# The input projection of a hybrid decoder trunk: one fp32 product becomes three float32r products, and the first tile follows the weights' pieces

## The chip, the cores and the metric

The kernel runs on one core of a Trainium2 chip. A core has five engines that run their own queues and meet at semaphores: TensorE (PE; its weight loads are shown apart as PEld), VectorE (DVE), ScalarE (ACT), GpSimd (POOL) and SyncE (SP, which here only issues transfers). The metric is the device time of one execution in microseconds. It is 4939.12 us before (median of three, 4939.12 to 4946.64).

## The reference, cut to what matters

One decoder layer runs over 2072 rows (16 meta tokens, 2048 prompt tokens, 8 sample rows). All rows first pass a layer norm and one projection:

```python
h = layer_norm(x, ln_emb_g, ln_emb_b)          # rows x 1024
qa, ka, va, qi, ki, wi, qb, kb, vb, fl = split(h @ w_in)   # 1024 x 2000
# then: rotary on qa, ka, qi, ki; log_sigmoid(fl + b_forget); cumulative sums of it
# sparse attention (indexer, top 256), forgetting attention, output product, gated feed-forward
```

The change is in `h @ w_in` alone. All arithmetic is float32 in the reference.

## The kernel before, in words

The program has five stages, each a block of its own with all engines meeting at its end: `project`, `attend`, `decode`, `mix_out`, `feed_forward`. The feed-forward stage already forms its products from operands split in two float32r parts (`three`, lines 1437 to 1442), as the changed projection does; the projection before uses plain fp32.

`project` walks over 17 tiles of 128 rows (`tiles`: tiles 0 and 1 written out, a hardware loop over pairs, and the last one). For a tile t:

- SP loads its rows to `x_in` once tile t-2 has left DVE (`x_free`) and its rows are stored (`h_stored`). At the start SP also loads `w_in` in eight pieces of 128 x 2000 (1 MB each), straight to their place, all issued in one go (line 203).
- DVE makes the layer norm (`norm`, lines 376 to 391), one tile ahead of the products.
- PE turns the normed rows (`turn_h`, eight transposes to `pT`), ACT copies them out (`copy_h`, line 354, to `hT`), and PE forms four chunks of 500 columns (`pP`), each the sum of eight products over the contraction (line 306). Behind chunk 1 stands `forget_sum` and behind chunk 2 `turn_q`, both for the tile before; behind chunk 3 stands `turn_h` for the next tile.
- ACT copies each chunk to `pn` (line 335), then `copy_h` of the next tile, then an Exp and a Ln (lines 342 and 344), with table loads.
- DVE adds the forget bias (`z`, `az`), applies the rotary steps (lines 427 to 432), and ends with line 434, which waits for ACT's Ln; that end is `lf_done` and `x_free`. `augment` (lines 393 to 404) comes behind the next norm; `turn_q` waits for it and for POOL's copies.
- POOL stores the normed rows, `pn` and the turned queries and keys.

So at a tile's boundary PE waits for ACT's `copy_h` of the next tile, and for nothing else; in tile 0 it waits for all eight pieces of the weights (`w_here`). Order within each engine is the order of the code.

Of the kernel before, what the change touches and what calls it, by code (L numbers as in the profile page):

```python
# [15 lines left out]
P = 128  # L16
D = 1024
KD = D // P
# [3 lines left out]
TILES = -(-ALL // P)  # L22
# [12 lines left out]
N_IN = 2000  # L35
PROJ_CHUNKS = 4
PROJ_W = N_IN // PROJ_CHUNKS
# [52 lines left out]
def project(nc, X, RT, W_IN, LN_G, LN_B, BF, CONST, PN, QTA, QTB, KTD, HN, keep):  # L90

    ident, ones = keep["ident"], keep["ones"]
    with ExitStack() as ctx:
        def sb(name, shape, dt=F32):
            return ctx.enter_context(nc.sbuf_tensor(name, shape, dt))

        def sem(name):
            return ctx.enter_context(nc.semaphore(name))  # L100

        w_in = sb("w_in", [P, KD, N_IN])
        tri = sb("tri", [P, P])
        kT = sb("kT_out", [P, 4, P])
        g_emb = sb("g_emb", [P, D])
# [1 line left out]
        bf = sb("bf", [P, HEADS])  # L107
        x_in = [sb(f"x_in{p}", [P, D]) for p in range(2)]
        rt = [sb(f"rt{p}", [P, 2 * ROPE]) for p in range(2)]
        hT = [sb(f"hT{p}", [P, KD, P]) for p in range(2)]  # L110
        pn = [sb(f"pn{p}", [P, N_IN]) for p in range(2)]
        rope_a = sb("rope_a", [P, 2, 9, ROPE])
        rope_b = sb("rope_b", [P, 2, 9, ROPE])
# [15 lines left out]
        pT = ctx.enter_context(nc.psum_tensor("pT", [P, 2, 512], F32))  # L129
        pP = ctx.enter_context(nc.psum_tensor("pP", [P, 4, 512], F32))  # L130
        pQ = ctx.enter_context(nc.psum_tensor("pQ", [P, 2, 512], F32))
        c_ps = pT[:, 0, 0:HEADS]

        w_here = sem("w_here")
        consts_here = sem("consts_here")
        x_here = [sem(f"x_here{p}") for p in range(2)]
        x_free = sem("x_free")
# [1 line left out]
        sd_done = sem("sd_done")  # L139
        h_done = sem("h_done")  # L140
        hT_ps = sem("hT_ps")
        hT_done = sem("hT_done")
        proj_ps = sem("proj_ps")
        pn_done = sem("pn_done")
        az_done = sem("az_done")
# [39 lines left out]
        @block.sync  # L185
        def _(sp):
            sp.dma_start(g_emb[:], LN_G.unsqueeze(0).to_broadcast([P, D])).then_inc(consts_here, 16)
            sp.dma_start(b_emb[:], LN_B.unsqueeze(0).to_broadcast([P, D])).then_inc(consts_here, 16)
            sp.dma_start(bf[:], BF.to_broadcast([P, HEADS])).then_inc(consts_here, 16)
            sp.dma_start(ident[:], CONST[0]).then_inc(consts_here, 16)  # L190
            sp.dma_start(tri[:], CONST[1]).then_inc(consts_here, 16)
            sp.dma_start(ones[:], CONST[2]).then_inc(consts_here, 16)

            def load(t, p, i):

                if not (isinstance(t, int) and t < 2):
                    wait_alone(sp, x_free, t - 1)
                    wait_alone(sp, h_stored[p], 16 * i)
                sp.dma_start(x_in[p][:], X[ds(t * P, P), :]).then_inc(x_here[p], 16)
                sp.dma_start(rt[p][:], RT[ds(t * P, P), :]).then_inc(x_here[p], 16)  # L200
                if is_first(t):
                    for k in range(KD):
                        sp.dma_start(w_in[:, k, :], W_IN[k * P:(k + 1) * P, :]).then_inc(w_here, 16)

            tiles(sp, load)

# [47 lines left out]
        @block.tensor  # L254
        def _(pe):
            def turn_h(t, p):

                pe.wait_ge(h_done, t + 1)
                if not is_first(t):
                    pe.wait_ge(hT_done, t)  # L260
                if not (isinstance(t, int) and t < 2):
                    pe.wait_ge(aug_done, t - 1)
                for k in range(KD):
                    ins = pe.transpose(pT[:, k // 4, (k % 4) * P:(k % 4 + 1) * P], x_in[p][:, k * P:(k + 1) * P], ident[:])
                ins.then_inc(hT_ps, 1)

            def turn_q(t, p):

                pe.wait_ge(kdup_done, t + 1)
                pe.wait_ge(aug_done, t + 1)  # L270
                for b in range(5):
                    if is_first(t) and b < 2:
                        pass
                    else:
                        pe.wait_ge(q_evac, t * 5 + max(b - 1, 0))
                    out = pQ[:, b % 2, :].rearrange("p (c n) -> p c n", c=4)
                    for c in range(4):
                        if b == 0:
                            ins = pe.transpose(out[:, c, :], pn[p][:, QA + c * P:QA + (c + 1) * P], ident[:])
                        elif b == 1:  # L280
                            ins = pe.transpose(out[:, c, :], pn[p][:, QI + c * P:QI + (c + 1) * P], ident[:])
                        elif b == 2 and c < 2:
                            ins = pe.transpose(out[:, c, :], kdup[:, c, :, :].rearrange("p a b -> p (a b)"), ident[:])
                        elif b == 2:
                            ins = pe.transpose(out[0:AUG, c, :], k_aug[:, c - 2, :], ident[:])
                        else:
                            ins = pe.transpose(out[0:AUG, c, :], q_aug[:, (b - 3) * 4 + c, :], ident[:])
                    ins.then_inc(q_ps, 1)

            def forget_sum(t, p):  # L290

                pe.wait_ge(lf_done, t + 1)

                pe.wait_ge(hT_done, TILES if is_last(t) else t + 2)
                pe.matmul(c_ps, tri[:], pn[p][:, FL:FL + HEADS], start=True, stop=False)
                pe.matmul(c_ps, ones[:], lf_sum[:], start=False, stop=True).then_inc(c_sum_ps, 1)

            def tile(t, p, i):
                pe.wait_ge(hT_done, t + 1)
                for j in range(PROJ_CHUNKS):  # L300
                    if not is_first(t):
                        pe.wait_ge(pn_done, (t - 1) * PROJ_CHUNKS + j + 1)
                    for k in range(KD):
                        if is_first(t) and j == 0:
                            pe.wait_ge(w_here, 16 * KD)
                        ins = pe.matmul(pP[:, j, 0:PROJ_W], hT[p][:, k, :], w_in[:, k, j * PROJ_W:(j + 1) * PROJ_W],  # L306
                                        start=(k == 0), stop=(k == KD - 1))
                    ins.then_inc(proj_ps, 1)
# [12 lines left out]
            turn_q(LAST, 0)  # L321

        @block.scalar
        def _(act):
# [25 lines left out]
            def copy_h(t, p):  # L350
                act.wait_ge(hT_ps, t + 1)
                if not (isinstance(t, int) and t < 2):
                    act.wait_ge(proj_ps, (t - 1) * PROJ_CHUNKS)
                act.activation(hT[p][:].rearrange("p a b -> p (a b)"), pT[:].rearrange("p a b -> p (a b)"),  # L354
                               ACT.Copy).then_inc(hT_done, 1)

            def copy_q(t):
                if not is_first(t):
# [9 lines left out]
            act.wait_ge(pool_init, 1 + HEADS)  # L368
            root(0)
            copy_h(0, 0)  # L370
            tiles(act, tile)
            copy_q(LAST)

        @block.vector
        def _(v):
            ch = Chain(v, dve)

            def norm(t, p, turn):
                v.wait_ge(x_here[p], 32 * (turn + 1))
                layer_norm_stats(ch, x_in[p], stats[:], mv[:])  # L380
                v.sem_inc(var_done, 1)
                v.wait_ge(sd_done, t + 1)
                ch.step(v.reciprocal(rs[:], sd[:]))
                ch.wait()
                ch.step(v.tensor_scalar(x_in[p][:], x_in[p][:], mv[:, 0:1], rs[:], ALU.subtract, ALU.mult))
                ch.wait()
                ch.step(v.tensor_tensor(x_in[p][:], x_in[p][:], g_emb[:], ALU.mult))
                ch.wait()
                ch.step(v.tensor_tensor(x_in[p][:], x_in[p][:], b_emb[:], ALU.add))
                ch.wait()  # L390
                v.sem_inc(h_done, 1)

            def augment(t):

# [14 lines left out]
            def tile(t, p, i):  # L409
# [9 lines left out]
                ch.step(v.scalar_tensor_tensor(out=az[:], in0=z[:], scalar=-1.0, in1=z[:], op0=ALU.mult, op1=ALU.max))  # L419
                ch.wait()  # L420
                v.sem_inc(az_done, 1)

                x4 = [pn[p][:, s:s + 9 * HD].rearrange("p (h d) -> p h d", d=HD) for s in (QA, QI)]
                cos = rt[p][:, 0:ROPE].unsqueeze(1).to_broadcast([P, 9, ROPE])
# [26 lines left out]
            v.wait_ge(consts_here, 96)  # L451
            v.wait_ge(pool_init, 1 + HEADS)
            norm(0, 0, 0)
            per = 2 * (2 + 1 + 4 + 4 + 1 + 1 + 6 + 2 + 1 + 2)
            tiles(v, tile, ch, per)
            augment_last = LAST
# [1918 lines left out]
```

## Time and profile before

| what | value |
| --- | --- |
| time, median of three runs | 4939.12 us (4939.12 to 4946.64) |
| the profiled execution's own time | 4938.44 us |
| its span, first to last instruction | 4936.8 us |
| PE busy | 4234.8 us (86%) |
| DVE / ACT / POOL busy | 2652.9 / 1742.7 / 604.8 us |
| mean granted TensorE clock | 0.917 of full |
| fp32 products of the projection (line 306), PE busy | 469.5 us |

The profile cuts the span in 40 slices of some 123 us. The projection fills nearly the first five: PE is busy 7, 9, 9, 9 and 7 tenths there, and its clock row reads 9 until the projection's end. A row of the trace's timeline reads: start in us, duration in us, engine, line, operation, output <- inputs, shape, count; in brackets how long the engine had been idle, and what ended that. A matmul's duration is a modelled one and overlaps its neighbour's; the distance from one start to the next is the pace. An fp32 product of line 306 leaves two matmul records, a float32r product one.

### The profile page before, as it was taken

To read this page: it belongs to the slowest core of one execution; us is meant where nothing else is said; L and a number is where in the kernel's file an instruction comes from. 1 tells how busy PE (TensorE), PEld (TensorE's weight loads), DVE (VectorE), ACT (ScalarE), POOL (GpSimd) and SP (SyncE) were. 2 spreads that over 40 slices of the span, in tenths; PEclk is the share of its full clock that TensorE was granted. 3 is DMA by queue.
4 is the path that set the end of the run, shared out by engine and by line. 5 is a ranking of instruction groups with operands and counts; after the bars stand their busy time and mean duration, and the time that the engine had idled before them with its cause. 6 is when DMAs were issued, how large, how long until landed. Compare 5 with 4: busy or idle time off the path is not lost. (4 is left out here: it accounts for less than half of the span.)

```text
span 4936.8 us, 61684 instructions
## 1 busy us (share of the span) xinstructions
PE 4234.8 (86%) x23278; PEld 3118.9 (63%) x23278; DVE 2652.9 (54%) x4961; ACT 1742.7 (35%) x2684; POOL 604.8 (12%) x695
## 2 busy tenths in 40 slices
PE   7999748777777888778787798797999999999997
PEld 3444324445555555455546544345999999999997
DVE  2222158989999999998423311343335344353533
ACT  2332223444444445444453344002323233232331
POOL 0221221100000000000167730000000000000000
PEclk9999956888889899999898888898999999999998
DMA  3322220000000000000277751334444534445442
GB/s 131 102 93 84 97 82 31 25 23 16 16 16 16 16 16 9 12 12 5 75 233 216 239 194 35 123 112 119 116 133 125 145 111 125 120 133 141 113 125 71
DMA packets 460722, 444.86 MB, mean 90 GB/s; under 512 B 26728, under 2 KB 405299, under 8 KB 460484
## 3 DMA queue, kind: packets, MB, share of 16 engines
q1 hardware_dynamic: 403396, 256.46, 18.3%
q0 software_dynamic: 57104, 185.42, 11.2%
q8 instruction: 142, 2.33, 0.2%
q14 instruction: 80, 0.66, 0.0%
HBM read 371.71 MB, written 69.95 MB: 89 GB/s over the span
## 5 line engine op out<-in xcount | busy, mean ns | idle before, releaser
L467 DVE TENSOR_SCALAR_CACHE_REDUCE at_relu<-at_scores,at_cand 128x272 f32<-128x272 f32 (+14 forms) x480 | 685.1, 1427 | 9.4
L1440 PE MATMUL ff_ps<-ff_h_high,ff_w_high 128*128 128x412 f32 x1760 | 619.3, 352 | 25.5 <-DVE ff_w_low L1534 25.5
L1441 PE MATMUL ff_ps<-ff_h_low,ff_w_high 128*128 128x412 f32 x1760 | 615.5, 350 | 0.0
L1442 PE MATMUL ff_ps<-ff_h_high,ff_w_low 128*128 128x412 f32 x1760 | 613.2, 348 | 0.0
L306 PE MATMUL pP<-w_in,hT 128*128 128x500 f32 x1088 | 469.5, 587 | 31.0 <-ACT hT L354 19.0
L1534 DVE TENSOR_TENSOR ff_w_low<-ff_w_raw,ff_w_high 128x2048 fp32r<-128x2048 f32 (+1 forms) x150 | 375.6, 2504 | 188.8 <-ACT ff_w_high L1489 188.6
L921 ACT ACTIVATE at_probs<-at_probs,at_nmax 128x144 f32<-128x144 f32 (+15 forms) x256 | 310.9, 1214 | 464.5 <-DVE at_nmax L1003 464.3
L1489 ACT ACTIVATE ff_w_high<-ff_w_raw 128x2048 fp32r<-128x2048 f32 (+1 forms) x150 | 311.5, 2076 | 360.1 <-PE ff_ps L1442 357.9
L934 ACT ACTIVATE at_pT_sb<-tr 128x512 f32<-128x512 f32 x544 | 304.0, 593 | 327.3 <-PE tr L807 326.8
L787 PE MATMUL S<-at_kbT,at_queries_b 73*128 73x512 f32 (+16 forms) x768 | 317.4, 556 | 116.8 <-DVE at_nmax L1003 64.4
L306 PEld LDWEIGHTS pP<-w_in,hT 128*128 128x128 f32 x1088 | 203.8, 191 | 263.4 <-issue 260.7
L807 PE MATMUL tr<-ident,at_probs 128*128 128x128 f32 x2176 | 340.5, 300 | 10.9 <-ACT at_pT_sb L934 5.7
L1440 PEld LDWEIGHTS ff_ps<-ff_h_high,ff_w_high 128*128 128x128 f32 x1760 | 331.1, 188 | 28.3 <-issue 26.2
L1442 PEld LDWEIGHTS ff_ps<-ff_h_high,ff_w_low 128*128 128x128 f32 x1760 | 330.7, 188 | 3.3
L1441 PEld LDWEIGHTS ff_ps<-ff_h_low,ff_w_high 128*128 128x128 f32 x1760 | 330.9, 188 | 0.7
L807 PEld LDWEIGHTS tr<-ident,at_probs 128*128 128x128 f32 x2176 | 278.7, 156 | 82.7 <-ACT at_pT_sb L934 44.8
L787 PEld LDWEIGHTS S<-at_kbT,at_queries_b 73*128 73x128 f32 x768 | 148.5, 215 | 265.8 <-issue 156.4
L1442 PE MATMUL ff_ps<-ff_hid_high,ff_w_low 128*128 128x412 f32 x880 | 308.1, 350 | 0.0
L1441 PE MATMUL ff_ps<-ff_hid_low,ff_w_high 128*128 128x412 f32 x880 | 308.0, 350 | 0.0
L1440 PE MATMUL ff_ps<-ff_hid_high,ff_w_high 128*128 128x412 f32 x880 | 308.0, 350 | 0.0
L2003 ACT ACTIVATE de_kT<-de_tr 128x512 f32<-128x512 f32 (+1 forms) x320 | 177.7, 594 | 330.2 <-PE de_tr L1816 329.4
L787 PE MATMUL S<-at_ka_high,at_q_a 128*128 128x512 f32 (+16 forms) x384 | 159.4, 417 | 132.1 <-DVE at_nmax L1003 128.6
(310 smaller groups left out, 6412.1 us busy)
## 6 DMA issues: line engine op xcount, KB each, us to landing
ff_w_raw<-in_w_gate SPq DMA_DIRECT2D x110, 512.0 KB, 4.0
ff_w_raw<-in_w_up SPq DMA_DIRECT2D x110, 512.0 KB, 5.2
ff_w_raw<-in_w_down SPq DMA_DIRECT2D x80, 704.0 KB, 5.8
out_PN<-pn POOLq DMA_DIRECT2D x17, 1000.0 KB, 6.2
at_q_raw<-dram_QTA SPq DMA_DIRECT2D x124, 128.0 KB, 2.8
x_in<-in_x_rows SPq DMA_DIRECT2D x17, 512.0 KB, 3.8
dram_HN<-x_in POOLq DMA_DIRECT2D x17, 512.0 KB, 8.0
dram_QTA<-qaiT POOLq DMA_DIRECT2D x17, 512.0 KB, 5.3
```

The costliest lines, as they stand in the source:

```text
L306: ins = pe.matmul(pP[:, j, 0:PROJ_W], hT[p][:, k, :], w_in[:, k, j * PROJ_W:(j + 1) * PROJ_W], start=(k == 0), stop=(k == KD - 1))
L467: return v.tensor_scalar(out, x, cand.bitcast(F32), 0.0, ALU.is_ge, ALU.add, accum_out=cnt)
L787: ins = pe.matmul(out[:, lo:lo + w], lhsT, rhs, start=(k == 0), stop=(k == len(passes) - 1))
L807: ins = pe.transpose(tr[state["tb"] % 2][:, h, :], of(h), ident[:])
L921: act.activation(row, row, ACT.Exp, bias=nmax[:, slot:slot + 1], scale=-1.0, accum_out=den[:, slot:slot + 1]).then_inc(exp_done, 1)
L934: act.activation(pT[:, n["pvs"].n % TURNED, :], tr[state["tb"] % 2][:].rearrange("p a b -> p (a b)"), ACT.Copy)\
L1440: pe.matmul(out, w_high[p][:, w], high, start=first, stop=False)
L1441: pe.matmul(out, w_high[p][:, w], low, start=False, stop=False)
L1442: return pe.matmul(out, w_low[p][:, w], high, start=False, stop=last)
L1489: act.activation(w_high[p][:, 0:cols], w_raw[p][:, 0:cols], ACT.Copy).then_inc(w_high_done, 1)
L1534: v.tensor_tensor(w_low[p][:, 0:cols], w_raw[p][:, 0:cols], w_high[p][:, 0:cols].bitcast(F32), ALU.subtract).then_inc(w_low_done, 1)
L2003: act.activation(kT[0:rows, slot, :], tr[0:rows, unit % 2, :], ACT.Copy).then_inc(tr_copied, 1)
```

## The change

- The weights are kept as two float32r parts, `w_high` and `w_low`. A piece is loaded to one of the two `pn` buffers, ACT copies it to `w_high` (a float32r copy), DVE subtracts to make `w_low`; then the buffer takes another piece. So pieces 0 and 1 are loaded at once, and each later piece when DVE has done the one two before it.
- The turned rows are split in the same way: `copy_h` writes `h_high`, and a new DVE step `lower` subtracts `h_high` from `pT` (still in PSUM) into `h_low`. Within a tile `lower(t + 1)` stands behind `az` and ahead of the rotary steps. PE now waits for `h_low_done`.
- Each fp32 product becomes three float32r products (high by high, high by low, low by high).
- In tile 0 the contraction is the outer loop: PE takes a piece for all four chunks as soon as that piece is split. Later tiles keep the chunk as the outer loop.
- In tile 0 the rows of tile 1 are loaded ahead of pieces 2 to 7; DVE and ACT split all the weights before they start tile 1's norm.

```diff
                 if is_first(t):
-                    for k in range(KD):
-                        sp.dma_start(w_in[:, k, :], W_IN[k * P:(k + 1) * P, :]).then_inc(w_here, 16)
+                    for k in range(2):
+                        load_w(k)
+                elif isinstance(t, int) and t == 1:
+                    for k in range(2, KD):
+                        sp.wait_ge(w_low_done, k - 1)
+                        load_w(k)
...
+            def three(p, k, j):
+                out, cols = pP[:, j, 0:PROJ_W], slice(j * PROJ_W, (j + 1) * PROJ_W)
+                pe.matmul(out, h_high[p][:, k, :], w_high[:, k, cols], start=(k == 0), stop=False)
+                pe.matmul(out, h_high[p][:, k, :], w_low[:, k, cols], start=False, stop=False)
+                return pe.matmul(out, h_low[p][:, k, :], w_high[:, k, cols], start=False, stop=(k == KD - 1))
+
             def tile(t, p, i):
-                pe.wait_ge(hT_done, t + 1)
+                pe.wait_ge(h_low_done, t + 1)
+                if is_first(t):
+
+                    for k in range(KD):
+                        pe.wait_ge(w_low_done, k + 1)
+                        for j in range(PROJ_CHUNKS):
+                            ins = three(p, k, j)
+                            if k == KD - 1:
+                                ins.then_inc(proj_ps, 1)
...
+            for k in range(KD):
+                act.wait_ge(w_here[k % 2], 16 * (k // 2 + 1))
+                act.activation(w_high[:, k], pn[k % 2][:], ACT.Copy).then_inc(w_high_done, 1)
+            act.wait_ge(w_low_done, KD)
             tiles(act, tile)
...
+            def lower(t, p):
+                v.wait_ge(h_high_done, t + 1)
+                v.tensor_tensor(h_low[p][:].rearrange("p a b -> p (a b)"), pT[:].rearrange("p a b -> p (a b)"),
+                                h_high[p][:].rearrange("p a b -> p (a b)").bitcast(F32), ALU.subtract).then_inc(h_low_done, 1)
...
                 v.sem_inc(az_done, 1)
+                if not is_last(t):
+                    lower(t + 1, 1 - p)
...
             norm(0, 0, 0)
+            lower(0, 0)
+            for k in range(KD):
+                v.wait_ge(w_high_done, k + 1)
+                v.tensor_tensor(w_low[:, k], pn[k % 2][:], w_high[:, k].bitcast(F32), ALU.subtract).then_inc(w_low_done, 1)
```

On PE, the end of tile 0 and the start of tile 1, before (`pT` takes the turned rows, `pP` the products):

```order
L306 MATMUL pP<-w_in,hT 128x500 x32
L264 MATMUL pT<-ident,x_in 128x128 x8
L306 MATMUL pP<-w_in,hT 128x500 x16
L295 MATMUL pT<-pn,tri 128x8
L296 MATMUL pT<-lf_sum,ones 128x8
L306 MATMUL pP<-w_in,hT 128x500 x8
```

and the same place in the change (each three rows are one product; `hT_high` and `hT_low` are the two parts of the rows):

```order
L314 MATMUL pP<-w_high,hT_high 128x500
L315 MATMUL pP<-w_low,hT_high 128x500
L316 MATMUL pP<-w_high,hT_low 128x500
L278 MATMUL pT<-ident,x_in 128x128 x8
L314 MATMUL pP<-w_high,hT_high 128x500
L315 MATMUL pP<-w_low,hT_high 128x500
L316 MATMUL pP<-w_high,hT_low 128x500
```

The transposes stand where they stood; 32 instructions a tile became 96.

On DVE, the end of tile 0, before:

```order
L417 TENSOR_TENSOR z<-pn,bf 128x8 [waits dve1,pn_done]
L419 SCALAR_TENSOR_TENSOR az<-z 128x8 [waits dve1]
L427 TENSOR_TENSOR rope_a<-pn,rt 128x144 [waits dve1]
L428 TENSOR_TENSOR rope_b<-pn,rt 128x9x8
L429 TENSOR_TENSOR rope_b<-pn,rt 128x9x8
```

and in the change:

```order
L451 TENSOR_TENSOR z<-pn,bf 128x8 [waits dve1,pn_done]
L453 SCALAR_TENSOR_TENSOR az<-z 128x8 [waits dve1]
L424 TENSOR_TENSOR hT_low<-pT,hT_high 128x1024 [waits dve1,h_high_done]
L463 TENSOR_TENSOR rope_a<-pn,rt 128x144
L464 TENSOR_TENSOR rope_b<-pn,rt 128x9x8
L465 TENSOR_TENSOR rope_b<-pn,rt 128x9x8
```

A subtraction of 1024 columns now stands between ACT's copy and PE's products, and ahead of the rotary steps.

On SP, the first loads (`pn` is the buffer that the pieces now pass through), before:

```order
L199 DMA x_in<-in_x_rows 128x1024
L200 DMA rt<-in_rope 128x32
L203 DMA w_in<-in_w_in 128x2000 x8
L199 DMA x_in<-in_x_rows 128x1024
L200 DMA rt<-in_rope 128x32
```

and in the change:

```order
L208 DMA x_in<-in_x_rows 128x1024
L209 DMA rt<-in_rope 128x32
L201 DMA pn<-in_w_in 128x2000 x2
L208 DMA x_in<-in_x_rows 128x1024
L209 DMA rt<-in_rope 128x32
L201 DMA pn<-in_w_in 128x2000 [waits w_low_done] x6
```

Six of the eight pieces now wait for DVE; the rows of tile 1 come ahead of them.

## Rows read from the trace of the kernel before

**Rows 1.** The page's first line: span and instructions.

```profile
span 4936.8 us, 61684 instructions
```

**Rows 2.** Timeline of PE, one tile: start, duration, instruction, [idle before, releaser].

```profile
193.69 13.68 PE L306 MATMUL pP<-w_in,hT 128*128 128x500 f32 x32 [1.20 <-ACT hT L354]
...
224.62 1.04 PE L264 MATMUL pT<-ident,x_in 128*128 128x128 f32 x8
226.86 0.68 PE L306 MATMUL pP<-w_in,hT 128*128 128x500 f32 x1 [1.20 <-ACT hT L354]
```

**Rows 3.** Timeline, ACT and DVE at the end of the same tile.

```profile
225.70 1.02 ACT L354 ACTIVATE hT<-pT 128x1024 f32<-128x1024 f32 x1 [0.28 <-PE pT L264]
...
229.89 0.17 DVE L434 SCALAR_TENSOR_TENSOR pn<-z,sp_l 128x8 f32<-128x8 f32 x1 [2.27 <-ACT sp_l L344]
```

**Rows 4.** Timeline of PEld, fp32 weight loads: first and last of 14.

```profile
208.07 0.19 PEld L306 LDWEIGHTS pP<-w_in,hT 128*128 128x128 f32 x1 [0.23 <-issue]
...
213.52 0.19 PEld L306 LDWEIGHTS pP<-w_in,hT 128*128 128x128 f32 x1 [0.23 <-issue]
```

**Rows 5.** Feed-forward's 412-column products: stretch, length, busy PE PEld DVE ACT, clock, DMA.

```profile
3500.00:3600.00 100.00, 100.00 (x535) 99.45 (x534) 6.41 (x11) 5.67 (x11) 1.00 0.46 123
```

**Rows 6.** Timeline of PE, attention: a 512-column float32r product and the next.

```profile
2407.54 0.39 PE L787 MATMUL S<-at_ka_low,at_q_a 128*128 128x512 f32 x1
2407.77 0.25 PE L787 MATMUL S<-at_ka_high,at_q_a 128*128 128x176 f32 x1
```

**Rows 7.** Instructions of three lines: duration in ns (min/median/max), first and last start, forms.

```profile
L1489 ACT ACTIVATE ff_w_high<-ff_w_raw x150: 1894/1902/2572, 3394.5 to 4878.3; 128x2048 fp32r<-128x2048 f32 x110, 128x2816 fp32r<-128x2816 f32 x40
L1534 DVE TENSOR_TENSOR ff_w_low<-ff_w_raw,ff_w_high x150: 2272/2293/3094, 3397.5 to 4880.9; 128x2048 fp32r<-128x2048 f32 x110, 128x2816 fp32r<-128x2816 f32 x40
L387 DVE TENSOR_TENSOR x_in<-x_in,g_emb x17: 1224/1226/1227, 13.1 to 536.2; 128x1024 f32<-128x1024 f32 x17
```

**Rows 8.** Timeline of the start, to the first product of tile 1.

```profile
15.75 1.94 PE L264 MATMUL pT<-ident,x_in 128*128 128x128 f32 x8 [15.75 <-DVEq L391]
...
17.73 1.02 ACT L354 ACTIVATE hT<-pT 128x1024 f32<-128x1024 f32 x1 [5.74 <-PE pT L264]
29.72 20.66 PE L306 MATMUL pP<-w_in,hT 128*128 128x500 f32 x43 [12.03 <-DMA w_in<-in_w_in]
31.05 1.29 DVE L84 BATCH_NORM_STATS2 stats<-x_in 128x6 f32<-128x512 f32 x2 [15.50 <-DMA rt<-in_rope]
...
35.31 1.23 DVE L389 TENSOR_TENSOR x_in<-x_in,b_emb 128x1024 f32<-128x1024 f32 x1
...
61.17 13.68 PE L306 MATMUL pP<-w_in,hT 128*128 128x500 f32 x32 [1.11 <-ACT hT L354]
```

**Rows 9.** DMA issues: output <- input, queue, count, KB each, us from issue to landing.

```profile
ff_w_raw<-in_w_gate SPq DMA_DIRECT2D x110, 512.0 KB, 4.0
ff_w_raw<-in_w_up SPq DMA_DIRECT2D x110, 512.0 KB, 5.2
...
out_PN<-pn POOLq DMA_DIRECT2D x17, 1000.0 KB, 6.2
...
w_in<-in_w_in SPq DMA_DIRECT2D x8, 1000.0 KB, 13.5
```

**Rows 10.** PE after two idle gaps; stretches: busy PE PEld DVE ACT POOL, clock.

```profile
731.15 0.59 PE L787 MATMUL S<-at_ka_high,at_q_a 128*128 128x272 f32 x1 [2.50 <-DVE at_nmax L1003]
...
2824.97 0.43 PE L1898 MATMUL de_pw<-de_lf_all,de_after 128*128 128x64 f32 x2 [2.38 <-DVE de_lf_all L2151]
...
61.20:594.30 533.10, 497.19 (x1532) 248.47 (x1532) 127.62 (x382) 162.86 (x241) 105.84 (x189) 1.00 0.27 91
...
730.90:737.60 6.70, 4.73 (x28) 3.24 (x28) 6.18 (x29) 2.85 (x9) 0.00 (x0) 0.50 0.00 0
...
2826.70:2830.00 3.30, 3.30 (x18) 3.30 (x17) 1.09 (x5) 0.00 (x0) 2.39 (x4) 0.50 0.91 300
```

**Rows 11.** Timeline of DVE: end of `augment` in the tile of rows 2.

```profile
208.84 0.16 DVE L402 TENSOR_TENSOR lf_sum<-lf_sum,pn 128x8 f32<-128x8 f32 x1
```

More of the change, by code:

```diff
@@ L100, in sem @@
             return ctx.enter_context(nc.semaphore(name))
-        w_in = sb("w_in", [P, KD, N_IN])
+        w_high = sb("w_high", [P, KD, N_IN], F32R)
+        w_low = sb("w_low", [P, KD, N_IN], F32R)
         tri = sb("tri", [P, P])
@@ L109, in project @@
         rt = [sb(f"rt{p}", [P, 2 * ROPE]) for p in range(2)]
-        hT = [sb(f"hT{p}", [P, KD, P]) for p in range(2)]
+        h_high = [sb(f"hT_high{p}", [P, KD, P], F32R) for p in range(2)]
+        h_low = [sb(f"hT_low{p}", [P, KD, P], F32R) for p in range(2)]
         pn = [sb(f"pn{p}", [P, N_IN]) for p in range(2)]
@@ L132, in project @@
         c_ps = pT[:, 0, 0:HEADS]
-        w_here = sem("w_here")
+        w_here = [sem(f"w_here{p}") for p in range(2)]
+        w_high_done = sem("w_high_done")
+        w_low_done = sem("w_low_done")
         consts_here = sem("consts_here")
@@ L141, in project @@
         hT_ps = sem("hT_ps")
-        hT_done = sem("hT_done")
+        h_high_done = sem("h_high_done")
+        h_low_done = sem("h_low_done")
         proj_ps = sem("proj_ps")
@@ L192, in _, with load_w @@
             sp.dma_start(ones[:], CONST[2]).then_inc(consts_here, 16)
+            def load_w(k):
+                sp.dma_start(pn[k % 2][:], W_IN[k * P:(k + 1) * P, :]).then_inc(w_here[k % 2], 16)
             def load(t, p, i):
@@ L259, in turn_h @@
                 if not is_first(t):
-                    pe.wait_ge(hT_done, t)
+                    pe.wait_ge(h_low_done, t)
                 if not (isinstance(t, int) and t < 2):
@@ L292, in forget_sum @@
                 pe.wait_ge(lf_done, t + 1)
-                pe.wait_ge(hT_done, TILES if is_last(t) else t + 2)
+                pe.wait_ge(h_low_done, TILES if is_last(t) else t + 2)
                 pe.matmul(c_ps, tri[:], pn[p][:, FL:FL + HEADS], start=True, stop=False)
                 pe.matmul(c_ps, ones[:], lf_sum[:], start=False, stop=True).then_inc(c_sum_ps, 1)
-            def tile(t, p, i):
-                pe.wait_ge(hT_done, t + 1)
+            def three(p, k, j):
[3 more added lines that the diff above has]
+                return pe.matmul(out, h_low[p][:, k, :], w_high[:, k, cols], start=False, stop=(k == KD - 1))
+            def tile(t, p, i):
+                pe.wait_ge(h_low_done, t + 1)
[6 more added lines that the diff above has]
+                                ins.then_inc(proj_ps, 1)
                 for j in range(PROJ_CHUNKS):
@@ L302, in tile @@
                         pe.wait_ge(pn_done, (t - 1) * PROJ_CHUNKS + j + 1)
[L303 to L308, printed above, removed]
+                        for k in range(KD):
+                            ins = three(p, k, j)
+                        ins.then_inc(proj_ps, 1)
                     if j == 1 and not is_first(t):
@@ L353, in copy_h @@
                     act.wait_ge(proj_ps, (t - 1) * PROJ_CHUNKS)
-                act.activation(hT[p][:].rearrange("p a b -> p (a b)"), pT[:].rearrange("p a b -> p (a b)"),
-                               ACT.Copy).then_inc(hT_done, 1)
+                act.activation(h_high[p][:].rearrange("p a b -> p (a b)"), pT[:].rearrange("p a b -> p (a b)"),
+                               ACT.Copy).then_inc(h_high_done, 1)
             def copy_q(t):
@@ L453, in _ @@
             norm(0, 0, 0)
+            lower(0, 0)
+            for k in range(KD):
+                v.wait_ge(w_high_done, k + 1)
+                v.tensor_tensor(w_low[:, k], pn[k % 2][:], w_high[:, k].bitcast(F32), ALU.subtract).then_inc(w_low_done, 1)
             per = 2 * (2 + 1 + 4 + 4 + 1 + 1 + 6 + 2 + 1 + 2)
```

## The prediction

> **What bounds the kernel now.** I read the page first [rows 1], then PE's timeline over the projection, then what ends PE's waits there, then rows of other stages that already run the operations which the change brings in. The projection is the first 0.6 ms of a 4936.8 us span, and inside it PE sets the pace: one tile starts its products at 193.69, the next at 226.86, so a tile takes 33.17 us, and the only idle time that the boundary shows is 1.20 us, waiting for ACT's copy [rows 2, 3]. The other engines wait for PE: DVE's last step of a tile waits 2.27 us for ACT, not the reverse [rows 3]. What shortens PE's tile therefore shortens the span, until something else comes late, and what lengthens the wait at the boundary lengthens it. In tile 0 the order is different: PE waits 12.03 us for the weights, starts at 29.72, and tile 1 starts at 61.17 [rows 8]. The granted clock is full from tile 1 to the projection's end: 1.00 over 533 us [rows 10].
>
> **The products.** An fp32 product leaves two records; their weight loads are 13 distances apart from 208.07 to 213.52, so a record takes 0.419 us and a product 0.838 [rows 4]. A tile's 32 products take 26.8 of the 33.17 us. The projection has no float32r product, so its price is bounded from both sides. From below: in feed-forward 535 of them with 412 columns fill 100 us, 0.187 each [rows 5]. From above: in attention one with 512 columns is followed by the next after 0.23 us [rows 6]. 500 columns lie 0.88 of the way, so I take 0.225, three for 0.675. (The bars' own durations, 0.39 us in rows 6, are not the pace; they overlap.) A tile gains 32 x (0.838 - 0.675) = 5.2 us; with the ends it is 8.9 and 4.7. Tiles 1 to 16 run this way: 16 x 5.2 = -83.5 us. The third weight load of each product costs nothing: at 412 columns loads are side by side with products for 99.45 of 100 us and the pace is still 0.187 [rows 5].
>
> The Trainium skill ("FP8 and Floating Point Precision", TensorE Precision Notes) says that true FP32 makes four passes through the array. By that rule three passes of four would gain a quarter, 6.7 us a tile and 107 us in all; the rows price a split pass slightly above half a record (0.225 against 0.210), so they give less, and the sum above goes by the rows.
>
> **The boundary.** Today: turned rows, ACT's copy of 1.02 us, then PE [rows 2, 3]. The change puts a DVE subtraction of 1024 columns behind the copy. DVE's multiply of that size takes 1.226, and half of feed-forward's 2048-column split 1.15 [rows 7]. With a hand-off of 0.05 I take 1.27 us, all on PE's path, because the next chunk needs the low part: the idle gap grows from 1.20 to 2.47 us. There are 16 boundaries; the one ahead of tile 1 is counted with tile 0 below, so 15 x 1.27 = +19.0. On DVE the rotary steps queue behind this wait. They are covered: the step that ends the tile waits 2.27 us for ACT already [rows 3], so `x_free`, the stores and the next loads move with ACT as before; without that cover they would be 1.3 us later, still far from PE.
>
> **The next late thing** would be `turn_q`, which needs `augment`. In this tile `augment` ends at 209.0, 15.3 us after the products started [rows 2, 11]. `turn_q` stands after 24 products and the forget sum, 20.7 us before and 24 x 0.675 + 0.4 = 16.6 now, and the norm's chain starts 1.27 us earlier relative to the products. That leaves 2.5 us: no wait, but little room.
>
> **The clock.** In the projection a 1.20 us idle gap stands at every boundary and the clock stays at full, 2.4 GHz [rows 2, 10]. Elsewhere in this trace longer gaps at full clock are followed by the half level, 1.2 GHz: behind a 2.50 us gap that ended at 731.15 the stretch 730.9 to 737.6 was granted 0.50, behind a 2.38 us gap that ended at 2824.97 the stretch 2826.7 to 2830.0 was, although PE was busy for all of the latter [rows 10]. Of eight gaps of 2.3 to 2.7 us (these are the first and the last) seven were followed by it within 4.5 us of their start. 2.47 us lies between those two rows, so I expect the change to lose the clock behind about 14 of the 16 boundaries. At half rate PE's work takes nearly twice the time (eight transposes 1.94 against 1.04 us) [rows 2, 8]. A stretch of 3.3 us costs 1.7 us, one of 6.7 costs 3.4; PE behind a boundary is as dense as in the shorter one, so I take 1.7: 14 x 1.7 = +23.8, from 0 up to 16 x 3.4 = +54.
>
> The Trainium skill ("TensorE: Matmul & The Clock Gate", Why this matters for your kernels) asks for no idle gaps above some 3 us between bursts of products; by that rule 2.47 us would be harmless, which is the first rival below. The trace speaks against it, with halves behind 2.38 and 2.50 us.
>
> **Tile 0.** Before, eight pieces in flight at once landed in time for a start at 29.72. Now a piece must pass through one of two buffers: load, ACT copy, DVE subtraction, next load. Copies of 2048 columns take 1.90 and subtractions 2.29 [rows 7], so 1.86 and 2.24 for 2000. A load of 1 MB: two of 512 KB issued together are there after 5.2; 4.0 (one alone) and 6.2 (1 MB from POOL) are the ends; 13.5 was behind all the others' bytes [rows 9]. With 0.3 of hand-offs a buffer turns round in 9.6 us. ACT is free for the first copy at 18.75 [rows 8]; DVE ends piece 0 at 22.9 and piece 1 at 25.15, and three rounds later piece 7 at 53.95. PE's twelve passes of a piece (2.7 us, 5.4 at half rate) hide in a round; only the last piece's stand alone, and tile 1's norm covers those: it now comes behind the weights on DVE, and takes 5.5 us (31.05 to 36.54) [rows 8], to 59.45. Then 0.2 + 1.04 transposes, 1.07 copy, 1.27 subtraction and 0.1: tile 1 starts at 63.1 against 61.17 = +2.0. So nearly all products of tile 0 hide under the loads, but the weights are ready 24 us later and the norm no longer hides. Ends: -1.6 and +5.0.
>
> **The sum.** 2.0 - 83.5 + 19.0 + 23.8 = -38.7. From the profiled execution's 4938.4 (span 4936.8 and 1.6 around it, 0.7 below the median of 4939.1) that gives 4899.7: I forecast 4900. Attention, decode and feed-forward keep their instructions; I count nothing for them.
>
> **The rivals.**
> - *The clock holds* (few gaps are followed by half rate). For it: the projection has never shown one, and a gap of this size without a drop exists, one in eight. Against: rows 10. It gives 4938.4 - 62.5 = 4876.
> - *Something else comes late*: loads of pieces slower than 6.2 us, or `augment` behind `turn_q` by 1 to 2 us a tile, on top of the forecast. Each 1 us a round costs 3, each 1 us of `turn_q` 16. For it: only 2.5 us of room, and loads of 13.5 us exist. It gives some 4912 to 4932.
> - *Slower: the half rate stays.* A tile has 5.2 - 1.27 = 3.9 us to lose, so the change loses from 7.8 us of half rate per tile on. At 17 us per tile it would be 16 x 8.5 - 83.5 + 19.0 + 2.0 = +73.5, 5012. Against: the dense stretch in rows 10 was at half for 3.3 us, and unbroken products follow each boundary for 10.8.
> - *It doesn't do what it says*: at 500 columns a pass costs 0.28 us or more. From there three passes cost the two records' 0.838, and the boundary, the clock and tile 0 are lost on top: 4938.4 + 45 = 4983 or worse. Against: 0.23 at 512 columns [rows 6].
>
> **How the numbers follow.** Forecast 0.60, alone 4888 to 4912 (a pass at 0.23 adds 8, a few drops fewer take 10 off, tile 0 moves by -4 to +3; these seldom add up). Clock holds 0.23 (4868 to 4888). Something late 0.11. Half rate stays 0.04, no gain of products 0.02. The range 4868 to 4918 holds the first two nearly whole and a third of the third. A difference of 0.2%, some 10 us, is about what a measurement can tell from none: faster 0.92, same 0.04, slower 0.04.
>
> **What would show it.** In the changed profile: passes 0.22 to 0.23 apart at full clock; a boundary gap of some 2.5 us released by DVE's `lower`; clock in the projection's slices below 0.95, with half-rate stretches right behind the boundaries; tile 1 starting near 63; tile periods of some 31 us (29.3 where the clock holds); `turn_q` never waiting for DVE. The forecast is wrong if the projection's clock reads 1.00 throughout (then 4876), if it is at half for over 7 us a tile, or if a pass costs over 0.24.

## The result, and the profile after

The changed kernel takes 4901.63 us (median of four runs, 4900.03 to 4903.88), the kernel before beside it 4941.37 (4939.12 to 4946.64). The ratio is 0.9917, with a 95% interval of 0.9903 to 0.9931. The forecast was 4900, in a range of 4868 to 4918.

The page of the changed kernel: its span, and TensorE's granted clock in 40 slices of some 123 us.

```profile
span 4902.2 us, 62806 instructions
...
PEclk9999767888888899898898887998999999999998
```

The span is 34.6 us shorter than in [rows 1] (the profiled execution, 4903.88, is the longest of the four). All of it comes from the projection: its last product ends at 553.80 instead of 589.40, 35.6 us earlier. Attention's first score follows 34.8 us earlier, the output product's first 37.0, feed-forward's first 35.4: behind the projection the lead stays within 3 us of what it was.

PE's timeline over one tile and into the next, which answers to [rows 2]; passes that repeat are left out.

```profile
183.94 1.04 PE L278 MATMUL pT<-ident,x_in 128*128 128x128 f32 x8
187.43 0.49 PE L314 MATMUL pP<-w_high,hT_high 128*128 128x500 f32 x1 [2.46 <-DVE hT_low L424]
...
188.93 0.62 PE L316 MATMUL pP<-w_high,hT_low 128*128 128x500 f32 x1
...
190.18 0.62 PE L316 MATMUL pP<-w_high,hT_low 128*128 128x500 f32 x1
...
192.03 0.39 PE L315 MATMUL pP<-w_low,hT_high 128*128 128x500 f32 x1
192.26 0.39 PE L316 MATMUL pP<-w_high,hT_low 128*128 128x500 f32 x1
...
205.62 0.39 PE L316 MATMUL pP<-w_high,hT_low 128*128 128x500 f32 x1
205.85 0.60 PE L293 MATMUL pQ<-ident,pn 128*128 128x128 f32 x4
...
218.34 0.49 PE L314 MATMUL pP<-w_high,hT_high 128*128 128x500 f32 x1 [2.46 <-DVE hT_low L424]
```

Three things are to be seen. The tile takes 218.34 - 187.43 = 30.91 us instead of 33.17. The idle gap at the boundary is 2.46 us instead of 1.20, and DVE's `lower` (line 424) ends it. And the passes have two paces: 188.93 to 190.18 is three distances of 0.417, 192.03 to 192.26 is one of 0.23 (0.227 is the median at full clock). The bars show it too, 0.62 us and 0.39. `turn_q` (line 293) follows the product before it without a wait.

PE's waits from 60 to 560 us by their releaser (total us, times, longest), the boundaries' line:

```profile
PE pP L314 <- DVE hT_low L424: 39.2, 16, 2.5
```

Before, the 16 boundaries waited 1.2 us each.

Stretches of the same trace: start and end, length, busy PE, PEld, DVE, ACT, POOL with counts, granted clock, DMA share, GB/s. The first is the projection from tile 1 on; the others lie ahead of tile 1's products, behind tile 2's boundary, over the rest of tile 2, and behind tile 3's boundary.

```profile
62.70:553.80 491.10, 440.55 (x2040) 361.42 (x2040) 143.51 (x390) 157.97 (x235) 106.40 (x188) 0.94 0.29 99
58.70:62.00 3.30, 1.63 (x8) 1.23 (x6) 0.74 (x2) 1.62 (x2) 0.00 (x0) 0.50 0.00 0
96.20:99.50 3.30, 3.30 (x10) 2.62 (x9) 0.17 (x1) 1.49 (x2) 2.44 (x8) 0.50 0.45 41
99.70:126.80 27.10, 23.75 (x119) 19.56 (x118) 8.93 (x24) 8.38 (x13) 4.09 (x4) 1.00 0.32 103
126.90:130.20 3.30, 3.30 (x10) 2.63 (x9) 0.30 (x2) 1.71 (x3) 1.79 (x6) 0.50 0.40 53
```

Where [rows 10] had 1.00 over the whole projection, the clock now reads 0.94: full inside a tile, at the half level behind the boundary, where PE is busy for all 3.30 us. Such a stretch stands behind 15 of the 16 boundaries. The sixteenth is the one ahead of tile 1, where the clock was at half already.

The boundary on ACT and DVE, which answers to [rows 3]:

```profile
185.01 1.02 ACT L379 ACTIVATE hT_high<-pT 128x1024 fp32r<-128x1024 f32 x1 [0.28 <-PE pT L278]
...
186.07 1.23 DVE L424 TENSOR_TENSOR hT_low<-pT,hT_high 128x1024 fp32r<-128x1024 f32 x1 [0.94 <-ACT hT_high L379]
...
189.20 0.17 DVE L470 SCALAR_TENSOR_TENSOR pn<-z,sp_l 128x8 f32<-128x8 f32 x1 [0.34 <-ACT sp_l L369]
```

The subtraction starts 0.04 us behind the copy and takes 1.23 us, all of it ahead of PE. DVE's last step of the tile still waits for ACT, but only 0.34 us instead of 2.27: the subtraction took 1.23 of that cover and DVE's wait for the copy the other 0.70.

The start, which answers to [rows 8]:

```profile
23.25 21.02 SPq L201 DMA_DIRECT2D pn<-in_w_in  x6
...
23.37 0.76 PE L314 MATMUL pP<-w_high,hT_high 128*128 128x500 f32 x1 [5.24 <-DVE w_low L493]
...
27.90 1.88 ACT L398 ACTIVATE w_high<-pn 128x2000 fp32r<-128x2000 f32 x1 [5.19 <-DMA pn<-in_w_in]
...
50.65 2.24 DVE L493 TENSOR_TENSOR w_low<-pn,w_high 128x2000 fp32r<-128x2000 f32 x1 [0.98 <-ACT w_high L398]
...
52.81 1.28 DVE L84 BATCH_NORM_STATS2 stats<-x_in 128x6 f32<-128x512 f32 x2
...
58.46 1.87 PE L278 MATMUL pT<-ident,x_in 128*128 128x128 f32 x8 [2.51 <-DVEq L420]
...
62.70 0.79 PE L314 MATMUL pP<-w_high,hT_high 128*128 128x500 f32 x1 [2.37 <-DVE hT_low L424]
```

Piece 2 is issued at 23.25 and split by ACT from 27.90 on, so a load of 1 MB took 4.65 us. The last piece is split at 52.8, the norm of tile 1 follows on DVE, and tile 1's products start at 62.70. PE began at 23.37, when five of the eight pieces had not been asked for, so nearly all of tile 0's products lie under the loads.

### The profile page after: what moved, and what is told of

It reads as the page before. It is cut to its first block and busy times, and to the rows that moved or that the text cites. A ratio compares the mean times of both kernels' runs of the same rounds, so it can differ in the third digit from the quotient of the medians.

```text
span 4902.2 us, 62806 instructions
## 1 busy us (share of the span) xinstructions
PE 4177.0 (85%) x23822; PEld 3246.5 (66%) x23822; DVE 2690.2 (55%) x4986; ACT 1756.2 (36%) x2692; POOL 606.5 (12%) x695
## 5 line engine op out<-in xcount | busy, mean ns | idle before, releaser
L827 PE MATMUL S<-at_kbT,at_queries_b 73*128 73x512 f32 (+16 forms) x768 | 307.1, 541 | 123.5 <-DVE at_nmax L1043 68.7
L314 PE MATMUL pP<-w_high,hT_high 128*128 128x500 f32 x544 | 229.6, 422 | 50.1 <-DVE hT_low L424 39.2
L1258 PE MATMUL mo_po<-w_o,mo_mixT 128*128 128x512 f32 x544 | 239.1, 598 | 24.0 <-DMA mo_h<-dram_HN 24.0
```

The costliest lines, as they stand in the source:

```text
L314: pe.matmul(out, h_high[p][:, k, :], w_high[:, k, cols], start=(k == 0), stop=False)
L827: ins = pe.matmul(out[:, lo:lo + w], lhsT, rhs, start=(k == 0), stop=(k == len(passes) - 1))
L1258: ins = pe.matmul(po[p][:, j * 512:(j + 1) * 512], mixT[p][:, k, :], w_o[:, k, j * 512:(j + 1) * 512], start=(k == 0), stop=(k == KD - 1))
```

## The experiments

The theory, with which the numbers expected below agree: 96 passes for 32 products give 5 us a tile back, `lower` costs 1.26 of them, and the longer gap costs some 25 us through the clock. The rivals: the passes gained less or more and something else made up for it; the lost clock costs nothing; the clock is lost because the passes are float32r, not because of the gap. Counts of falls to the half level are those of the one profiled execution of each kernel.

### The passes that need only the high part first

Chunk 0 of tiles 1 to 16 does its 16 passes on `h_high` first and its 8 on `h_low` last. PE then waits for ACT's copy as before, and `lower` runs beside the 16 passes.

```diff
+            def high_first(p, t):
+                for k in range(KD):
+                    pe.matmul(out, h_high[p][:, k, :], w_high[:, k, cols], ...)
+                    pe.matmul(out, h_high[p][:, k, :], w_low[:, k, cols], ...)
+                pe.wait_ge(h_low_done, t + 1)
+                for k in range(KD):
+                    ins = pe.matmul(out, h_low[p][:, k, :], w_high[:, k, cols], ...)
...
-                pe.wait_ge(h_low_done, t + 1)
+                pe.wait_ge(h_low_done if is_first(t) else h_high_done, t + 1)
```

> The changed kernel, except that from tile 1 on chunk 0 takes its sixteen passes with the high part of the rows first (they need only ACT's copy) and its eight passes with the low part behind them; PE waits for DVE's subtraction there, 3.6 us of passes later. Theory (the boundary costs 1.26 us of subtraction and, through the 2.46 us gap, some 1.45 us of half clock): the gap is back at 1.2 us, the granted clock reads 1.00 over the projection, a tile takes 28.2 us instead of 30.9, and the time is 4901.6 - 16 x 2.7 = 4858. Rival 1 (the half clock comes with float32r passes as such, not with the gap): only the subtraction is hidden, a tile takes 29.6, the clock record still falls once a tile, 4881. Rival 2 (something else at the boundary sets the pace): no change, 4902.

Measured: 4858.56 us (4855.06 to 4861.85), ratio to the kernel before 0.984 (0.9823 to 0.9856). PE, ACT and DVE at two boundaries, then the stretch from tile 1 to the projection's end:

```profile
201.80 1.02 ACT L392 ACTIVATE hT_high<-pT 128x1024 fp32r<-128x1024 f32 x1 [0.29 <-PE pT L278]
202.85 1.23 DVE L437 TENSOR_TENSOR hT_low<-pT,hT_high 128x1024 fp32r<-128x1024 f32 x1 [0.94 <-ACT hT_high L392]
202.96 0.49 PE L321 MATMUL pP<-w_high,hT_high 128*128 128x500 f32 x1 [1.20 <-ACT hT_high L392]
...
231.07 0.49 PE L321 MATMUL pP<-w_high,hT_high 128*128 128x500 f32 x1 [1.20 <-ACT hT_high L392]
```

```profile
62.00:509.70 447.70, 415.91 (x2038) 342.23 (x2036) 143.31 (x390) 157.91 (x236) 105.88 (x188) 1.00 0.32 108
```

The gap is the old one, 1.20 us, the clock reads 1.00 (only tile 1 begins at the half level, granted 0.50 from 61.0 to 64.4, which the mean hides), and the tile takes 231.07 - 202.96 = 28.11 us. Against 33.17 at the same gap and the same clock that is the price of the products alone: 5.06 us a tile, 81 in all. Of the change as it stands, 44 us (553.80 - 509.74, the ends of the last product) went to one wait.

### The gap filled with products for nothing

How much of the 44 us is the clock and how much the longer path? Nine passes into a bank that nobody reads stand in the gap; the wait for `lower` stays.

```diff
             def tile(t, p, i):
+                if not is_first(t):
+                    ...
+                    for n in range(9):
+                        pe.matmul(pQ[:, 1, 0:PROJ_W], h_high[1 - p][:, n % KD, :], w_high[:, n % KD, 0:PROJ_W], ...)
                 pe.wait_ge(h_low_done, t + 1)
```

> The changed kernel, except that PE does nine passes for nothing (to a free bank of PSUM) at each boundary while it waits for the subtraction; the wait itself stays where it was. Theory: the subtraction still costs its 1.26 us, but the clock no longer falls: a tile takes 29.4 to 29.6 us instead of 30.9, 4901.6 - 16 x 1.4 = 4879. Rival 1 (the half clock comes with float32r passes as such): falls stay, no gain, 4902 or some us more where the nine passes reach beyond the wait. Rival 2 (a fall costs the full 3.4 us of its stretch, hidden elsewhere in my sum): 4847.

Measured: 4876.55 us (4875.01 to 4881.08), ratio 0.9881 (0.9864 to 0.9897). PE at a boundary, then the projection from tile 1 on:

```profile
235.27 1.03 PE L278 MATMUL pT<-ident,x_in 128*128 128x128 f32 x8
236.06 2.29 PE L323 MATMUL pQ<-w_high,hT_high 128*128 128x500 f32 x9
238.76 0.49 PE L314 MATMUL pP<-w_high,hT_high 128*128 128x500 f32 x1 [0.41 <-DVE hT_low L429]
```

```profile
62.00:528.00 466.00, 445.83 (x2176) 365.81 (x2175) 143.98 (x391) 158.58 (x236) 105.83 (x188) 1.00 0.31 104
```

PE's idle gap is 0.41 us, the path through `lower` is what it was, and the clock reads 1.00. The last product ends 25.1 us earlier (528.70). So 25 of the 44 us are the clock and 19 the path (16 x 1.26 = 20, less some 1.5 that tile 1's half level costs the kernel with the high passes first). The forecast of 4876 for "the clock holds" is this kernel, to within a microsecond.

### Plain fp32 products with the longer gap

Does the gap alone cost the clock? The kernel before gets the same subtraction at the same place, into a buffer that nobody reads, and PE waits for it; no operand is split.

```diff
+            def lower(t, p):
+                v.wait_ge(hT_done, t + 1)
+                v.tensor_tensor(waste[:], pT[:]..., hT[p][:]..., ALU.subtract).then_inc(waste_done, 1)
...
+                if not is_last(t):
+                    lower(t + 1, 1 - p)
...
-                pe.wait_ge(hT_done, t + 1)
+                pe.wait_ge(waste_done, t + 1)
```

> The kernel before (fp32 products, weights loaded as before), with one DVE subtraction of 1024 columns put between ACT's copy and PE's products; its result is used by nobody. Theory (the gap alone makes the clock fall): a boundary's gap grows to 2.46 us, the clock falls to half once a tile, each tile costs 1.26 + 1.5 to 1.7 more, 4941.4 + 16 x 2.85 = 4987. Rival 1 (the falls belong to the float32r passes): the clock stays at 1.00, only the subtraction is added, 4941.4 + 16 x 1.26 = 4962.

Measured: 4959.96 us (4958.99 to 4961.99), ratio 1.0049 (1.0032 to 1.0065). The theory said 4987 and failed; the rival's 4962 holds. What PE waited for in the projection (total us, times, longest), and stretches as above: the projection, behind one boundary, behind the next.

```profile
PE pP L308 <- DVE waste L397: 39.2, 16, 2.5
```

```profile
62.60:613.00 550.40, 499.81 (x1528) 249.21 (x1528) 142.82 (x390) 157.96 (x236) 106.53 (x188) 0.99 0.26 88
270.50:273.80 3.30, 3.30 (x6) 1.30 (x5) 0.17 (x1) 1.58 (x2) 1.92 (x7) 0.50 0.39 63
305.20:308.50 3.30, 3.30 (x8) 1.62 (x9) 1.56 (x9) 2.99 (x4) 0.49 (x1) 1.00 0.04 6
```

All 16 gaps are there, 39.2 us in all, as in the changed kernel. But only 2 of them are followed by the half level. Each of these two makes its tile 36.13 us long instead of 34.43, so 1.70 for one fall, the price taken in the forecast. The same gap is lost 15 times in one kernel and twice in another: either fp32 products keep the clock where float32r ones don't, or it hangs on when the gap comes, since the tile is 3.5 us longer here. Two runs tell these apart: each makes the tiles of one kernel longer by work far from the boundary, and leaves the gap and what lies around it as they are.

### Longer tiles, the same gap

The changed kernel gets 16 passes for nothing behind chunk 0 of tiles 1 to 16 (3.6 us a tile).

```diff
+                    if j == 0 and not is_first(t):
+                        ...
+                        for n in range(16):
+                            pe.matmul(pQ[:, 1, 0:PROJ_W], h_high[p][:, n % KD, :], w_high[:, n % KD, 0:PROJ_W], ...)
```

> The changed kernel with sixteen passes for nothing (to a free bank of PSUM) behind chunk 0 of tiles 1 to 16: the gap of 2.46 us and the operations around it stay, only the tile grows by 16 x 0.227 = 3.6 us. It asks why float32r lost the clock at 16 of 16 boundaries and fp32 with the same gap at 2 of 16. Reading A (a gap between float32r passes loses the clock every time): 16 falls, tile 30.9 + 3.6 = 34.5 us, time 4901.6 + 58 = 4960. Reading B (it depends on when the gap comes, and tiles of 30.9 us happened to meet the same moment again and again): falls at some boundaries only, 6 to 13 of 16, tiles of 33.1 and of 34.6 mixed, 4945 to 4955.

Plain fp32 with the longer gap, as above, gets two fp32 products for nothing at the same place (1.7 us a tile).

```diff
+                        for n in range(2):
+                            pe.matmul(pQ[:, 1, 0:PROJ_W], hT[p][:, n % KD, :], w_in[:, n % KD, 0:PROJ_W], ...)
```

> The kernel before with the unused DVE subtraction at the boundary (2.46 us of gap), and two fp32 products for nothing behind chunk 0 of tiles 1 to 16: the same gap, tiles 1.7 us longer. Reading A (between fp32 products a gap of 2.46 us mostly keeps the clock, whenever it comes): again 0 to 4 falls of 16, 4960 + 27 = 4987 and up to 4 us more. Reading B (it depends on when the gap comes): a clearly different number of falls, 8 or more, each costing 1.6 us, 5000 or more.

Measured, one run each: 4950.60 and 5008.49 us. The changed kernel with 16 more passes, PE at two boundaries, then the projection and the stretches behind the two:

```profile
200.53 0.78 PE L314 MATMUL pP<-w_high,hT_high 128*128 128x500 f32 x1 [2.46 <-DVE hT_low L429]
...
234.88 0.49 PE L314 MATMUL pP<-w_high,hT_high 128*128 128x500 f32 x1 [2.46 <-DVE hT_low L429]
```

```profile
61.60:606.00 544.40, 493.88 (x2296) 406.02 (x2296) 143.08 (x390) 158.08 (x235) 105.20 (x188) 0.96 0.27 89
200.20:203.50 3.30, 2.97 (x7) 2.47 (x8) 1.89 (x10) 3.24 (x5) 0.15 (x1) 0.50 0.00 0
234.90:238.20 3.30, 3.30 (x15) 2.75 (x16) 1.55 (x9) 2.97 (x4) 0.52 (x1) 1.00 0.02 5
```

Plain fp32 with two more products, the same two views:

```profile
248.26 8.43 PE L308 MATMUL pP<-w_in,hT 128*128 128x500 f32 x16 [2.46 <-DVE waste L402]
...
285.83 4.45 PE L308 MATMUL pP<-w_in,hT 128*128 128x500 f32 x10 [2.45 <-DVE waste L402]
```

```profile
61.60:657.00 595.40, 544.85 (x1591) 268.94 (x1592) 143.11 (x390) 158.05 (x235) 105.99 (x188) 0.96 0.24 81
247.90:251.20 3.30, 2.94 (x4) 1.45 (x5) 1.92 (x10) 3.24 (x5) 0.14 (x1) 0.50 0.00 0
285.90:289.20 3.30, 3.30 (x8) 1.55 (x9) 1.49 (x9) 2.92 (x4) 0.56 (x2) 1.00 0.07 6
```

In each kernel one gap of 2.46 us is followed by half the clock and another of the same length, between the same operations, is not. Over the projection the counts are 13 of 16 for the first and 14 of 16 for the second. So plain fp32 products go from 2 falls to 14 when the tile grows by 1.7 us at a place far from the gap: not the kind of product decides, but when the gap comes. That is reading B of both expectations. The added work as such does not explain it: with more of it the changed kernel has fewer falls, 13 for 15, and plain fp32 has more. What in the gap's moment decides was not tried. Nor was a second execution of these two kernels; the four runs of plain fp32 with the longer gap lie within 3 us, so its count of 2 can hardly have varied much, as a fall there costs 1.70.

### Tile 0 with the chunk as the outer loop

```diff
-                    for k in range(KD):
-                        pe.wait_ge(w_low_done, k + 1)
-                        for j in range(PROJ_CHUNKS):
+                    pe.wait_ge(w_low_done, KD)
+                    for j in range(PROJ_CHUNKS):
+                        for k in range(KD):
```

> The changed kernel with the second part of the change undone: tile 0 waits for all eight split pieces and takes them chunk by chunk, as later tiles do. Theory: the weights are split at 52.8 us as in the changed kernel; then 96 passes take 21.8 us and some 2.3 more for a start at half clock, where before only the norm's 5.7 us followed. Tile 1 starts near 53 + 24 + 3.5 = 80 to 81 instead of 62.7, time 4901.6 + 18 = 4919. Rival (the weights' loading and splitting gets faster without PE reading them, by over 3 us): 4913 or less.

Measured: 4920.89 us (4918.90 to 4924.41), ratio 0.9958 (0.9943 to 0.9973). PE's first products in tiles 0 and 1:

```profile
53.45 0.76 PE L314 MATMUL pP<-w_high,hT_high 128*128 128x500 f32 x1 [35.33 <-DVE w_low L492]
81.21 0.49 PE L314 MATMUL pP<-w_high,hT_high 128*128 128x500 f32 x1 [2.37 <-DVE hT_low L423]
```

PE waits 35.33 us for the last piece, and tile 1 starts 18.5 us later than in the changed kernel. The order of the pieces is worth those 18.5 us at tile 1; by the medians, half of the gain would be gone without it. A part comes back behind tile 1: its first boundary is followed by no half level (the other 15 are), tile 1 takes 29.17 us instead of 31.98, and the projection ends 14.1 us later (567.88 against 553.80).

### Four buffers for the pieces, alone and with the high passes first

Two more buffers of 128 x 2000 take pieces, so that four are in flight. The second kernel adds the edit of the first experiment.

```diff
+        stage = pn + [sb(f"stage{p}", [P, N_IN]) for p in range(2)]
...
-                sp.dma_start(pn[k % 2][:], W_IN[k * P:(k + 1) * P, :]).then_inc(w_here[k % 2], 16)
+                sp.dma_start(stage[k % NS][:], W_IN[k * P:(k + 1) * P, :]).then_inc(w_here[k % NS], 16)
```

> The changed kernel with four buffers instead of two for the weights' pieces, the boundary left as it is. Theory: tile 1 starts at 50 to 51 instead of 62.7, 4901.6 - 12 = 4890; the half clock behind the boundaries stays. Rival (what is won in tile 0 is given back because the boundaries come at other moments): -12 in tile 0, and a number of falls other than 16, each fall less worth 1.5 us: down to 4870.

> The order of the high passes as in the run with high passes first, and four buffers instead of two for the weights' pieces on their way (two new ones beside the two of the projection's results), so four pieces are loaded at once. Theory: in tile 0 DVE's subtractions of 2.24 us follow each other from 21 us on and end near 39.5 instead of 52.8, so that now PE's 96 passes from 23.4 on (21.8 us, and some 2.3 for a start at half clock) end last, near 47.5; tile 1 starts near 50 instead of 62.7. With the boundary's gain: 4858 - 12 = 4846. Rival (the loads share one limit, so four at once bring the last piece no earlier): tile 1 starts at 61 or later, 4857.

Measured: four buffers alone 4891.15 us (4885.47 to 4893.27), ratio 0.9893 (0.9876 to 0.9910); both edits 4847.27 us (4843.42 to 4848.29), ratio 0.9816 (0.9800 to 0.9833). With four buffers alone, the last piece's subtraction and tile 1's start:

```profile
37.74 2.24 DVE L495 TENSOR_TENSOR w_low<-stage,w_high 128x2000 fp32r<-128x2000 f32 x1 [0.16 <-ACT w_high L400]
...
50.39 0.50 PE L316 MATMUL pP<-w_high,hT_high 128*128 128x500 f32 x1 [2.37 <-DVE hT_low L426]
```

The last piece is split 12.9 us earlier, and tile 1 starts at 50.39. Its load still waits for a buffer, but DVE now stands still less: its eight subtractions take 19.4 us from first start to last end (20.53 to 39.98) instead of 31.9 (20.98 to 52.89), 17.9 of them work. The half level follows all 16 boundaries, so the rival does not hold. With both edits, tiles 1 and 2 and the stretch from there:

```profile
49.22 0.49 PE L323 MATMUL pP<-w_high,hT_high 128*128 128x500 f32 x1 [1.11 <-ACT hT_high L394]
...
77.25 0.49 PE L323 MATMUL pP<-w_high,hT_high 128*128 128x500 f32 x1 [1.21 <-ACT hT_high L394]
```

```profile
50.00:496.00 446.00, 414.44 (x2037) 341.15 (x2036) 143.58 (x391) 158.44 (x236) 105.99 (x188) 1.00 0.32 108
```

The two gains add up: 28 us a tile, full clock, and the earlier start. Of the kernels that form all three passes it is the fastest, ahead of both that were given.

### Two passes instead of three

The first experiment's order with two passes a product (high by high and low by low; the mixed products are left out). It asks what is late next.

```diff
-                pe.matmul(out, h_high[p][:, k, :], w_low[:, k, cols], start=False, stop=False)
-                return pe.matmul(out, h_low[p][:, k, :], w_high[:, k, cols], ...)
+                return pe.matmul(out, h_low[p][:, k, :], w_low[:, k, cols], ...)
```

> The run with high passes first, with two passes a product instead of three (high by high, and low by low in place of the two mixed passes, so the two mixed products are left out of the result). It prices a pass in place and asks what comes late next. Theory: 32 passes less save 32 x 0.227 = 7.3 us of PE a tile, but turn_q would then be ready 11.4 us after the products started, while augment ends 13.9 us after them, driven by the load and the norm of the next rows. So PE waits some 2.5 us a tile for DVE: a tile of 23.3 to 23.5 us instead of 28.1, 4858.6 - 16 x 4.7 = 4783, and up to 25 us more if that wait costs the clock. Rival (norm and augment move up with PE): 20.9 us a tile, 4743.

Measured: 4821.27 us (two runs, 4817.69 and 4824.85), ratio 0.9759 (0.9717 to 0.9801). What PE waited for in the projection, and the projection's clock:

```profile
PE pQ L293 <- DVEq L449: 47.5, 15, 7.4
...
PE pQ L301 <- DVEq L496: 13.2, 15, 3.0
```

```profile
60.00:460.00 400.00, 320.71 (x1508) 260.77 (x1508) 143.38 (x389) 159.49 (x235) 106.94 (x188) 0.92 0.36 120
```

The wait that the forecast named as the next late thing, `turn_q` (line 293) for `augment`, appears: 47.5 us over 15 tiles, up to 7.4 in one. The mechanism holds; its size was missed by 38 us, or 13 with the clock's price, since a wait is 3.2 us in the mean but up to 7.4 in single tiles, a second one of up to 3.0 follows (line 301), and the clock falls to 0.92 as well. With three passes that room was enough, with two it is not.

## Why the prediction was right

Its terms, measured over tiles 1 to 16 and tile 0:

| term | forecast, us | measured, us | from |
| --- | --- | --- | --- |
| products, a tile | -5.2 | -5.06 | 33.17 - 28.11, same gap and clock |
| products, 16 tiles | -83.5 | -81.0 | |
| boundaries, 15 | +19.0 | +18.9 | gap 1.20 to 2.46 |
| clock | +23.8 | +25 | tile periods; 25.1 with the gap filled |
| tile 0 | +2.0 | +1.5 | 61.17 to 62.70 |
| sum | -38.7 | -35.6 | last product 589.40 to 553.80 |

- **The products.** A pass takes 0.227 us where 0.225 was taken, between the two neighbours in [rows 5, 6]. The third weight load costs nothing, as forecast. The four-pass rule of the Trainium skill ("FP8 and Floating Point Precision", TensorE Precision Notes) would have given 107 us; the runs show 81. So the row's price was the better one: a quarter of an fp32 product, 0.210 us, is less than a pass takes here.
- **The boundary.** Right to 0.01 us, and the reason too: filling the gap leaves this term in place, doing the high passes first removes it.
- **The clock.** The size was right, its working only in part. Falls: 15, where 14 were forecast. A fall costs 1.54 us in tiles 2 to 10 (30.91 - 33.17 + 5.06 - 1.26), 1.37 in tiles 11 to 15, less than the 1.7 taken; tile 1, which starts at half, loses 2.8. Together 25. What failed is the reason for the count: "2.47 us lies between those two rows" takes the length of the gap for what decides. Plain fp32 with gaps of 2.46 us lost the clock only twice. The moment of the gap decides too, and the prediction asked nothing about it. Six kernels here have this gap: five lost the clock at 13 to 16 boundaries, one at 2. So a count near 14 was likely but not sure, and to that extent its coming out was luck. The sample behind it also had nine gaps, not eight: the one left out, 2.37 us at the projection's own end (it ended at 596.55), came with the half level from 0.15 us after its start. The rule of the Trainium skill on idle gaps above some 3 us ("TensorE: Matmul & The Clock Gate", Why this matters for your kernels) doesn't hold here: 15 gaps below it were followed by the half level, and the 25 us return when they are filled.
- **The cover on DVE.** It held, but by less than written: the last step of the tile waits 0.34 us for ACT, not some 1.0, because `lower` also waits 0.94 us for the copy while the rotary steps queue behind it.
- **Tile 0.** From issue to ACT's copy the six later pieces took 4.6 to 4.8 us, one 5.4, instead of 5.2, and the hand-offs of a round hardly 0.1 instead of 0.3, so the last piece was split at 52.8, not 53.95. The transposes at half clock took 1.87 us instead of 1.04 and gave 0.8 of that back.
- **The rivals.** The clock did not hold; where it was made to hold, the time was the rival's 4876. Nothing else came late: PE's wait at line 293 for `augment` does not occur with three passes. The two losing cases did not occur.

The measured terms add up to the projection's gain, but the clock's 25 is what the tile periods leave when the other two terms are taken off; the check on it is the 25.1 of the kernel with the gap filled. The medians differ by 39.7 us, some 4 more than the projection shows in the two profiled executions; runs of one kernel spread by as much, so that remainder is not explained.

## What to carry to other kernels

Where a product becomes several passes, do first those that need only what is ready, and let the work for the rest run beside them: here one wait of 1.26 us a tile cost 44 us in all. Cost a longer idle gap on TensorE twice, once as path and once as clock, and look at the granted clock behind it; the second was the larger here. When operands have to be prepared on their way in, order the products by the pieces, and count how many buffers the pieces need.

## What had not been expected of the hardware

An idle gap of TensorE of one length, between the same operations, keeps the clock or loses it depending on when it comes: gaps of 2.46 us were followed by half rate 2 times of 16 in tiles of 34.43 us, 14 of 16 in fp32 tiles of 36.11 (without a fall), 13 of 16 in tiles of 32.98, 15 of 16 in the changed kernel, and 15 and 16 of 16 in the two kernels that change its tile 0 alone (chunk as the outer loop, four buffers). Gaps of 1.20 us lost it at none of the 15 boundaries from tile 2 on, in the kernel before as in the one with the high passes first. A fall lengthens the tile and with it moves the next gap, so falls are no independent events.
